# Feed-forward stages that multiply the unnormed residual, with ScalarE rounding their weights

## What is computed

```python
def rmsnorm(x, g):
    y = x * lax.rsqrt(jnp.mean(x * x, axis=-1, keepdims=True) + EPS)
    return y * g

def conv_glu_ffn(x, w_up, conv_w, conv_b, w_down):        # D_FF = 2816, FFN_CONV = 3
    h = causal_depthwise_conv(x @ w_up, conv_w, conv_b)
    gate, val = jnp.split(h, 2, axis=-1)
    return (jax.nn.silu(gate) * val) @ w_down

h = h + mixer(rmsnorm(h, mix_norm))
h = h + conv_glu_ffn(rmsnorm(h, ffn_norm), ffn_up, ffn_conv_w, ffn_conv_b, ffn_down)
```

## Time and profile before

| | |
|---|---|
| three runs | 2708.23, 2708.68, 2712.85 us; median 2708.68 |
| profiled execution | 2706.43 us; its span, first to last instruction, 2704.4 us |
| PE busy | 2591.5 us, 96% of the span |
| DVE, POOL, ACT busy | 1629.3 us (60%), 1148.9 us (42%), 638.8 us (24%) |
| entries of the feed-forward stages | at 180.4 and 821.1 us |
| attention loop | 1933.3 to 2067.0 us |

### The profile page before, as it was taken

One profiled execution on the slowest core, in us unless ns is written; L12 is line 12 of the kernel. 1 busy time (PEld: TensorE's weight loads), 2 busy tenths in 40 slices (PEclk: granted clock), 3 DMA queues, 4 the chain that ended last, 5 costly groups with the idle time before them and its releaser, 6 DMA issues. The chain is left out here.

```text
span 2704.4 us, 46228 instructions
## 1 busy us (share of the span) xinstructions
PE 2591.5 (96%) x19018; PEld 2176.9 (80%) x19018; DVE 1629.3 (60%) x2499; ACT 638.8 (24%) x1244; POOL 1148.9 (42%) x934
## 2 busy tenths in 40 slices
PE   8999999989899999999999989989899999999998
PEld 6778888878678888888798879876788888788887
DVE  7848848573457847857665566544676426562451
ACT  4212102110332201123543244322354100110000
POOL 3534555445324555433532253212332545454552
PEclk9999999999999999999999999999999999999999
DMA  4224334222023334321101110111111222232222
GB/s 161 94 109 137 122 138 143 91 94 94 16 78 132 131 113 161 112 85 63 42 31 37 71 40 27 34 37 51 52 26 47 94 94 95 76 104 99 94 94 78
DMA packets 51319, 229.73 MB, mean 85 GB/s; under 512 B 5296, under 2 KB 12480, under 8 KB 32576
## 3 DMA queue, kind: packets, MB, share of 16 engines
q1 hardware_dynamic: 51136, 227.10, 24.5%
HBM read 224.91 MB, written 2.17 MB: 84 GB/s over the span
## 5 line engine op out<-in xcount | busy, mean ns | idle before, releaser
L246 POOL TENSOR_TENSOR ring_rounded<-ring,ring_rounded 128x512 fp32r<-128x512 f32 (+2 forms) x711 | 929.0, 1338 | 1089.0 <-DVE ring_rounded L237 1076.4
L293 PE MATMUL psum<-arena_rounded,ring_rounded 128*128 128x512 f32 (+1 forms) x2820 | 1094.4, 388 | 39.9 <-DVE arena_rounded L569 11.8
L294 PE MATMUL psum<-arena_rounded,ring_rounded 128*128 128x512 f32 (+1 forms) x2820 | 1085.3, 385 | 0.0
L295 PE MATMUL psum<-arena_rounded,ring_rounded 128*128 128x512 f32 (+1 forms) x2820 | 1084.7, 385 | 0.0
L293 PEld LDWEIGHTS psum<-arena_rounded,ring_rounded 128*128 128x128 f32 x2820 | 532.5, 189 | 159.5 <-issue 30.5
L295 PEld LDWEIGHTS psum<-arena_rounded,ring_rounded 128*128 128x128 f32 x2820 | 532.5, 189 | 106.7
L294 PEld LDWEIGHTS psum<-arena_rounded,ring_rounded 128*128 128x128 f32 x2820 | 532.7, 189 | 102.8 <-issue 1.0
L237 DVE CAST ring_rounded<-ring 128x2048 fp32r<-128x2048 f32 (+4 forms) x191 | 213.1, 1116 | 637.5 <-PE psum L295 576.1
L723 ACT ACTIVATE arena<-psum,vectors 128x512 f32<-128x512 f32 x88 | 68.5, 781 | 406.6 <-PE psum L295 406.6
L336 DVE TENSOR_TENSOR arena_rounded<-arena,arena_rounded 128x512 fp32r<-128x512 f32 (+1 forms) x111 | 123.4, 1111 | 3.8
L334 DVE CAST arena_rounded<-arena 128x512 fp32r<-128x512 f32 (+1 forms) x111 | 109.1, 982 | 9.2 <-DVE arena L753 1.0
(11 more groups left out here) (411 smaller groups left out, 3097.9 us busy)
## 6 DMA issues: line engine op xcount, KB each, us to landing
ring<-in_w_up SPq DMA_DIRECT2D x44, 1024.0 KB, 4.8
arena<-in_w_mod SPq DMA_DIRECT2D x48, 512.0 KB, 3.5
ring<-in_w_down SPq DMA_DIRECT2D x32, 704.0 KB, 4.1
ring<-in_w_mup SPq DMA_DIRECT2D x16, 1024.0 KB, 4.8
ring<-in_w_mdown SPq DMA_DIRECT2D x16, 1024.0 KB, 4.8
ring<-in_w_gdn SPq DMA_DIRECT2D x12, 1024.0 KB, 4.8
ring<-in_w_lru_in SPq DMA_DIRECT2D x10, 1024.0 KB, 4.8
ring<-in_w_odd_in SPq DMA_DIRECT2D x10, 1024.0 KB, 4.8
```

The source lines that it names most:

```text
L246: last = pool.tensor_tensor(self.rounded(low), raw, self.rounded(high).bitcast(F32), ALU.subtract)
L293: pe.matmul(out, r(wh), r(xh), start=start, stop=False)
L294: pe.matmul(out, r(wh), r(xl), start=False, stop=False)
L295: return pe.matmul(out, r(wl), r(xh), start=False, stop=stop)
```

## The change

1. In the stages before a feed-forward stage (`lru_stage`, `odd_out_stage`), `Residual` gets a `norm`: for the first six tiles of `h`, ACT multiplies by the gain and rounds, DVE makes the remainder, and the squares are summed, all between the last stage's own units. DVE adds the tile t=0 of a unit to `h` as soon as that tile is done. Tiles 6 and 7 (`HELD = 6`) are left to the feed-forward stage. The hold at the end is 8 matmuls instead of 13.
2. `ffn_stage` has no norm ahead of its products. `first_unit` runs the six ready tiles, sums the squares, and runs the last two; `second_unit` spreads the root behind its first product. ACT copies the root's row to SBUF, and DVE multiplies both PSUM banks of every up unit by it in place (`scaled`), each as soon as its tile is done.
3. In up units ACT, not DVE, rounds the weights (`act_unit`) and the unit's result (`acthigh`); the first of the two modulation reductions goes between the two `scaled`, the second ahead of the remainder (behind it in the last unit).
4. In attention ACT rounds the next head's keys in step 0 and its turned keys in step 1.

```diff
+    def act_unit(self, act, unit):
+        nxt, slot = self.ahead(unit), unit.slot
+        act.wait_ge(self.raw_full[slot], (unit.use + 2) * 16)
+        act.activation(self.rounded(self.ring[:, 1, slot, 0:nxt[0].size]), ..., ACT.Copy).then_inc(self.hi_done, 1)
...
+    def dve_normed_unit(self, dve, unit):
+        for tile in range(2 * unit.u - 2, 2 * unit.u):
+            if tile >= 0:
+                self.norm.dve_low(dve, tile)
+            if tile >= 1:
+                self.add_square(dve, tile, unit, 0)
+        for t in range(2):
+            dve.wait_ge(m.sem("done"), m.count("done", self.done0 + tile + 1))
+            if t:
+                m.dve_unit(dve, unit)
+            dve.tensor_tensor(m.h[:, tile, :], m.psum[:, 2 * unit.slot + t, :], m.h[:, tile, :], ALU.add)...
...
     def pe(pe):
-        npe(pe)
+        def first_unit(unit):
+            for k in range(KD):
+                if k >= HELD:
+                    pe.wait_ge(m.sem("xready"), m.count("xready", k + 1 - HELD))
+                ...
+                if k == HELD - 1:
+                    pe.wait_ge(m.sem("normsummed"), m.count("normsummed", KD - HELD))
+                    norm.pe_sums(pe)
+        def second_unit(unit):
+                    if (t, k) == (0, 0):
+                        norm.pe_spread(pe)
...
     def act(act):
-        nact(act)
+        for k in range(HELD, KD):
+            norm.act_high(act, k)
+        for k in range(HELD, KD):
+            act.activation(sq[:, k - HELD, :], m.h[:, k, :], ACT.Square)...
         mod.act_begin(act)
+        norm.act_row(act)
...
+                    if t == 0:
+                        act.wait_ge(m.sem("done"), m.count("done", f0 + unit.u * 2 + 2))
+                        act.wait_ge(m.hi_done, unit.g + 2)
+                        m.act_unit(act, unit)
...
+                act.wait_ge(m.sem("gated"), m.count("gated", before + 1))
+                act.activation(m.rounded(pick(ah, unit.u)), pick(al, unit.u), ACT.Copy)...
...
-                m.dve_unit(dve, unit)
+                scaled(0)
+                mod.dve_first(dve, unit, half, True)
+                scaled(1)
+                tap(0)
+                tap(1)
...
-        m.hold(pe, 13, 5)
+        m.hold(pe, 8, 5)
...
                 if b == 0:
                     queries(h + 1)
+                    keys(h + 1)
                 if b == 1:
-                    keys(h + 1)
-                if b == 2:
                     turned_keys(h + 1)
```

More of the change, by code:

```diff
@@ L501, in dve_end @@
     def dve_end(self, dve):
-        if self.squares:
+        if self.squares and not self.norm:
             self.add_square(dve, KD - 1, Unit(self.seg, self.seg.n - 1, 0, 0, 1), 0)
@@ L506, in act_unit @@
         if not self.squares:
+            return
+        if self.norm:
+            self.act_normed_unit(act, unit)
             return
```

142 lines of the change are left out of this document (109 added, 33 removed).

## The result

The changed kernel takes **2689.8 us** (median of five runs, 2685.7 to 2692.7) where the kernel before takes 2708.2 (five runs, 2704.3 to 2712.9): a ratio of 0.9932, interval 0.9917 to 0.9946. The prediction said 2687, with 2680 to 2698. The profiled execution took 2688.2, its span 2686.1 against 2704.4: 18.3 us less, where the sum had 21.5.

The account below looks back on a forecast made before the run. TensorE (PE), busy 96% of the span, was taken as the bound. Entries 13.2, up to down 1.1 and attention 7.2 sum to 21.5 off 2706.4, giving 2684.9; the median lies 2.3 higher, so 2687 us, range 2680 to 2698.

Parts of the forecast that it names:

- The entries: Start of both feed-forward stages: third up unit 7.0 to 7.7 us earlier; 6.6 saved each, 13.2 for both.
- the lag: First half of up units: DVE trails PE by half a unit when the loop begins, costing 0 to 1.2 us.
- The norm's work in the stage before: Rounding, remainder and squares of six tiles between down units, costed at nothing; about 0.7 us if late by one tile.
- Up to down: Turn from up to down units: the 0.55 us wait at the third down unit is covered, twice, saving 1.1.
- Attention: Attention loop: earlier key rounding removes seven of PE's eight waits for turned keys, saving 7.2 us; head 0's stays.
- rival (c): Attention: keys' rounding overruns ACT's 0.89 us gap, the exponential is later at each head; 2694 us, chance 0.06.
- The steady up units: Steady run of up units: PE bounds at 10.9 us, DVE's cycle is 9.2 to 10.2, so net 0.
- rival (a): Up units: in-place multiplies are dear, 1.8 us each, DVE's cycle 11.9, total 2731 us; chance 0.08.
- the charge for meeting POOL: Up units: DVE operations stretch beside POOL, 0.36 us for the second reduction and 0.6 for the remainder.
- the sum's 8.34: Up units: DVE's busy time per unit, 9.53 − 2.55 + 1.36 = 8.34 us, without roundings, with two in-place multiplies.
- rival (b): Up units: DVE is paced by POOL, overrunning 0.1 to 0.35 us per unit; 2692 to 2702 us, chance 0.11.
- A clock drop: PE at half clock for a stretch: no new drop expected at the entries; one more or fewer worth about 3.4 us.

Follow-up runs that it names:

- the second trace: The changed kernel run once more with no edit: 2691.2 us against 2705.5 for the kernel before, ratio 0.9941.
- after: The changed kernel itself, against the kernel before: 2689.8 us against 2708.2, ratio 0.9932.
- red_early: Changed kernel with the second modulation reduction right behind the first, except in a half's last unit: 2691.3 us, 0.9934 of the kernel before.

## Why the prediction was right, and where its steps failed

**The entries: right.** Forecast 6.6 each net of the lag, and 0.55 at the third down unit, 7.15 in all; measured 7.5 per stage (371.83 to 364.33). By the steps: the first up product, forecast 2.0 behind the end of the last, comes 2.08 behind it; the third unit, forecast 7.0 to 7.7 earlier, comes 7.04 earlier, held up by POOL's weights as worked out; the lag cost 0.45 in the first half, within the 0 to 1.2. Barrier, holds, sums and spread amid the products all stood as told. The norm's work in the stage before, put at nothing, costs little: the products of `odd_out_stage` take 44.74 from first to last instead of 44.40 (45.09 in the second trace).

**Up to down: right in kind, a little small.** The wait at the third down unit is gone, and the first half's down units take 60.07 instead of 60.95: 0.88 against 0.55.

**Attention: right in size, and it is paid back in part at times.** Seven waits of 1.0 to 1.1 are gone. The loop without clock drops is 7.0 shorter, forecast 7.2; 0.8 of the 7.0 is busy time that the step did not count, and it hides what the step missed. What it overlooked is head 0: there ACT has no idle 0.89 ahead of the second exponential, so it comes later, and the turned keys' rounding waits 1.5 for DVE ahead of the third; PE's wait for the copied probabilities grows from 1.6 to 2.4, which is rival (c) at one head. One or two clock drops, in some runs, take another 1.6 to 2.9. The step read one head of the steady run and took it for all.

**The steady up units: the result right, the step wrong.** The price of the multiply in place was right, 0.69 against 0.68: rival (a) falls. The cycle was to be 9.2 to 10.2 and is 10.35 outside the loop and 11.11 within. The step that failed is the charge for meeting POOL. It took 0.36 for the second reduction and 0.6 for the remainder. Measured in the loop are 2.31 − 1.22 = 1.09 for the reduction, nothing for the remainder (0.69, as before), and 1.77 − 1.13 = 0.64 for the gate product, for which the step added nothing to what it took before. These 1.73 on the sum's 8.34 are DVE's 10.06 of busy time in a loop cycle, and gaps of 1.05 make 11.11. Ahead of the loop the remainder does stretch (1.66) and the gate product less (0.8 to 0.9). The rule that the prediction had weighed, from the Trainium skill ("SBUF — State Buffer", section "SBUF: two separate sides"), picks the right instructions: those with two SBUF inputs stretch beside POOL, the multiplies (0.69) and the taps (0.75) with an operand in PSUM do not. Most taps lie beside POOL's pieces in after, and in red_early nine multiplies do, at 0.68 to 0.70. The prediction named the mechanism as rival (b), with an overrun of 0.1 to 0.35 per unit, and gave it 0.11. The overrun is there, 0.2 per unit, but only in the loop, and costs 0.45 in a first half instead of 4 to 15 in all. After six units the loop ends, and DVE makes up 0.5 in each unit outside it: of PE's units the third, tenth and eleventh take 11.02, 11.06 and 11.01 instead of 10.88, and the up units of the second half take as long as before. Net 0 was thus luck of the loop's length as much as slack.

**What was not in the sum at all.** 5.3 us (8.5 in the second trace) went in the delta scans, in code that the change does not touch, for the most part because PE's program became 161 instructions shorter ahead of them (PE executes 80 matmuls and 80 weight loads fewer): 3.1 of the 5.3 are PE's "issue" waits (3.9 against 0.8). One more stretch at the lower clock is in the second scan; how the rest divides between it and what the waits delay is not shown. The prediction put changes at unchanged places at nothing but the clock; that term was missing. So 21.5 became 18.3: 5.3 went in the scans and 1.8 in the attention loop, the feed-forward stages gave 0.7 more than forecast, and 3.2 came at other places, most of it with less time at the lower clock. No step forecast these 3.2, and that the total came within 3 us of 2687 owes as much to luck. A clock drop, put at 3.4, costs 1.2 to 1.6 where it can be told apart, in the attention loop. The working's own bounds are also added wrongly: its least gains (10 − 0.8 + 5 − 3.4) reach 2698, not the 2693 that it gives. The range on record, 2680 to 2698, takes that in.

## What to carry to other kernels

When a norm's root can be applied behind the product, the entry of a stage falls to a barrier, but the next thing that is late is the chain behind the root: let nothing stand behind it that does not need it, here the rounding of weights. Where DVE and POOL share the work of a loop, place DVE's instructions with two SBUF inputs where POOL is idle; their order alone moved the cycle from 11.1 to PE's own 10.9. And after an edit compare the stages that it did not touch: a few us there, at a bound engine, may come from where its program now lies, and are neither credit nor debit of the edit.

## What the runs showed of the hardware

PE can stand still for 0.3 to 1.7 us amid like matmuls without any wait for a semaphore, at places that in part repeat from run to run and that move when instructions are added or taken far ahead of them: 0.6 to 2.0 us of "issue" waits in the two scans with PE's program at one place, 3.9 to 6.6 at others. That PE's program decides it, the runs with 161 more PE instructions show. That it is the loading of PE's instructions, their DMA packets show: 41 of 41 such waits over 0.3 us end 2.2 to 2.95 us after a packet of 16,384 bytes, 256 instructions, starts. Why the place decides which packets come late, no run here settles. An instruction that holds nothing but waits that are long fulfilled costs PE 0.11 us when many stand in a row (8.6 us more for 161 of them, with 9 us of idle time used up first).
